# A hybrid decoder trunk in fp32 on one core: the order of ScalarE's work inside a slot, and of two masks on GpSimd

## The chip, the cores and the metric

The kernel runs on one core of one Trainium2 chip. The metric is the device time of one execution in microseconds (us), the median of some runs. Five engines with a queue each do the work: TensorE (PE in the profile; its weight loads are PEld), VectorE (DVE), ScalarE (ACT), GpSimd (POOL) and SyncE (SP), which here only issues DMAs. Each engine takes its instructions strictly in program order, and they wait for each other by semaphores: an instruction that waits holds back everything behind it on its own engine.

## The reference

Two layers over 256 tokens of width 1024. In each, one input projection feeds three mixers, and then comes a gated MLP:

```python
for l in range(DEPTH):                       # DEPTH = 2
    h = rms_norm(x, norm_mix[l])
    proj = h @ w_in[l]
    u_ssm, q_nsa, kv_nsa, g_nsa, qkv_sb, g_merge = split_columns(proj)
    o_ssm = s5_mixer(u_ssm, ...)             # A: complex diagonal state space, a scan over the tokens
    o_nsa = nsa_mixer(q_b, k_b, v_b, ...)    # B: softmax attention, compressed/selected/window branches
    o_sb  = stick_breaking_attention(...)    # C: see below
    gate = sigmoid(g_merge)                  # one gate of width 1024 for each mixer
    x = x + (sum(gate * (branches @ w_branch[l])) @ w_out[l])
    x = x + conv_ffn(rms_norm(x, norm_ffn[l]), ...)
return rms_norm(x, norm_final)

# mixer C, for each of 8 heads; causal is k < q
log_rest = where(causal, log_sigmoid(-z), 0)
after = cumsum(log_rest, reverse=True) - log_rest
w = where(causal, exp(log_sigmoid(z) + after), 0)
out = w @ v
```

## The kernel before

**Products in fp32 by halves.** A weight piece of 128 x 1024 numbers is split into a high half on ScalarE (`split_hi`, line 1278, `wh<-ring`) and the rest on VectorE (`split_lo`, line 1576, `wl<-ring,wh`). TensorE then multiplies high by high, high by low and low by high. A semaphore `w_lo` tells TensorE that a piece is there, `w_used` tells ScalarE that one of the three piece buffers is free again.

**Units and banks.** The results of the input projection come as units in two PSUM banks, `pj0` for even units and `pj1` for odd ones. ScalarE empties a bank with `copy_out` (line 1265), which raises `unit_out`; TensorE can't start the next unit in that bank before. The units named `sbv` and `gate` are "wide": two slots of TensorE's work each fill `pj0` and `pj1` together, so their two copies come only at the end of every fourth slot.

**Slots.** The middle of a layer is a loop `for q in range(SLOTS)` with 56 slots, written out in the same order for each engine. In a slot TensorE does one "filler" (a piece of the projection, 12 matmuls of 512 columns for a wide one; from slot 36 on half of that of the branch projections), and then what tables of slot numbers put there for the mixers. The tables that matter here:

- Mixer B: `NSA_S` scores on TensorE, one slot later `NSA_X` the maxima on VectorE (`nm`) and the exponentials on ScalarE (line 1367), then `NSA_R` the scaling (line 1378), `NSA_T` transposes on TensorE, `NSA_C` their copy on ScalarE.
- Mixer A (S5): `S5_X` inputs on TensorE, `S5_T` turns on VectorE and GpSimd, `S5_G` a scan on VectorE and `s5_back` on GpSimd (line 2169), `S5_Y` outputs on TensorE (line 1091), which wait for the `s5_back` of four groups.
- Mixer C works on four pairs of heads, k = 0 to 3. `SB_Z` (slots 25, 29, 34, 39): scores into `bA` and `bB`. `SB_A`, a slot later: Abs (line 1395), Exp (1398) and Ln (1400) on ScalarE. `SB_P`, again a slot later: the sum on VectorE (`kr<-bA,work`) and the first mask on GpSimd (`kr<-kr`, line 2177). `SB_R` (slots 28, 32, 38, 42): TensorE's cumulative sum (`bA<-kr,kon`). `SB_M`, a slot later: the exponential of the weights on ScalarE (line 1384). `SB_D`: the second mask, on the weights, on GpSimd (`work<-work`, line 2177). `SB_O` (slots 30, 34, 40, 44): values on TensorE (`pj<-work,sbv`), which wait for that mask.

In ScalarE's slot the order is: `split_hi`, the copies of mixer B, then the exponentials and scalings of mixer B, `SB_M`, `SB_A`, and last, in odd slots, the `copy_out` of a unit that has just been filled. In GpSimd's slot it is: first mask, second mask, turns, `s5_back`. The table of the second mask puts it in the slot of `SB_M`, and for k = 0 one slot earlier, in slot 28, which has an `s5_back` behind it:

```python
SB_M = {s + 1: k for s, k in SB_R.items()}
SB_D = {s - (k == 0): k for s, k in SB_M.items()}
```

ScalarE evaluates Exp and Tanh from one function table, Ln from another; an `ACT_TABLE_LOAD` stands where it changes between them.

Of the kernel before, what the change touches and what calls it, by code (L numbers as in the profile page):

```python
# [21 lines left out]
ACT = mybir.ActivationFunctionType  # L22
# [7 lines left out]
NT = T // P  # L30
EPS = 1e-6
HD = 64
SCALE = HD ** -0.5
# [66 lines left out]
U_VG, U_K, U_Q, U_U, U_FILL = 0, 2, 4, 6, 8  # L100
# [31 lines left out]
SB_M = {s + 1: k for s, k in SB_R.items()}  # L132
SB_O = {s + 2: k for s, k in SB_R.items()}

SB_D = {s - (k == 0): k for s, k in SB_M.items()}

S5_X = {4 + (7 * p + 1) // 2: p for p in range(ST // 2)}
S5_T = {s + 1: p for s, p in S5_X.items()}
# [86 lines left out]
def build(nc, x, norm_mix, w_in, ssm_lam_re, ssm_lam_im, ssm_log_step, ssm_b_re, ssm_b_im,  # L225
# [3 lines left out]
    with ExitStack() as ctx:  # L229
# [54 lines left out]
        sbq = sb("sbq", [P, JC, T])  # L284
        sbk = sb("sbk", [P, 4, T])
        sbv = sb("sbv", [P, NT, CH])
        gate = sb("gate", [P, 3 * KD, T])
# [242 lines left out]
        def half(h):  # L530
            return slice(CH * h, CH * h + CH)
# [701 lines left out]
        def _(a):  # L1233
# [26 lines left out]
            def copy_out(l, n, dst, func=ACT.Copy, scale=1.0):  # L1260

                t, k = summed(n)
                a.wait_ge(t.sem, t.at(l, k))
                src = unit(n) if len(dst.shape) == 3 else pj[n % 2][:, :]
                A(dst, src, func, scale=scale).then_inc(unit_out[n % 2].sem, unit_out[n % 2].up())  # L1265
# [16 lines left out]
            for l in range(DEPTH):  # L1282
# [61 lines left out]
                for q in range(SLOTS):  # L1344
# [7 lines left out]
                    if q in NSA_C:  # L1352
                        r = NSA_C[q]
                        m = ROUNDS[r]
                        a.wait_ge(t_done.sem, t_done.at(l, r + 1))
                        if m:
                            a.wait_ge(v_done.sem, v_done.at(l, m))
                        A(pT[:, r % 3 // 2, :], bO[:, :], ACT.Copy).then_inc(t_ready.sem, t_ready.up())
                    if q in NSA_X:
                        m = NSA_X[q]  # L1360
                        w = nsa_pair(m)[2]
                        a.wait_ge(s_max.sem, s_max.at(l, m + 1))
                        for s in range(2):
                            for b in range(2):
                                p = pr[:, m % 2, s, w * b:w * b + w]
                                n = 2 * s + b
                                ins = A(p, p, ACT.Exp, bias=nm[:, m % 2, n:n + 1], scale=-1.0,  # L1367
                                        accum_out=sm[:, m % 2, n:n + 1])
                        ins.then_inc(s_exp.sem, s_exp.up())
# [16 lines left out]
                    if q in SB_A:  # L1386
# [11 lines left out]
                        A(w, w, ACT.Exp, scale=-1.0).then_inc(z_exp.sem, z_exp.up())  # L1398
                        a.wait_ge(z_exp.sem, z_exp.at(l, k + 1))
                        A(w, w, ACT.Ln, bias=1.0).then_inc(z_ln.sem, z_ln.up())  # L1400
                    if q % 2:
                        kind, *at = FILL[f]
                        if kind == "sbq":
                            copy_out(l, U_FILL + f, sbq[:, 2 * at[0]:2 * at[0] + 2, :], scale=SCALE)
                        elif kind == "sbk":
                            copy_out(l, U_FILL + f, sbk[:, 2 * at[0]:2 * at[0] + 2, :])
                        elif kind == "sbv":
                            for t in range(at[0] * NT):
                                copy_out(l, U_FILL + f - 1 + t, sbv[:, t, :])
                        elif kind == "glu":  # L1410
                            o = oS[:, 2 * at[0]:2 * at[0] + 2, :]
                            copy_out(l, U_FILL + f, o, ACT.Tanh, 0.5)
                        elif kind == "gate":
                            b, i = at
                            for t in range(i % 2 * NT):
                                copy_out(l, U_FILL + f - 1 + t, gates[:, b, t, half(i // 2)], ACT.Tanh, 0.5)
                    if q == GELU:
                        a.wait_ge(y_used.sem, y_used.at(l, JC))
                        A(yT[:, :, :], yT[:, :, :], ACT.Gelu_apprx_tanh).then_inc(y_ready.sem, y_ready.up())
# [834 lines left out]
```

## Time and profile before

| | us |
|---|---|
| median of 3 runs | 988.85 (988.18 to 989.59) |
| profiled execution, its own time | 989.32 |
| its span, first to last instruction | 987.6 |
| busy: TensorE, VectorE, ScalarE, GpSimd | 948.0, 777.8, 590.2, 340.3 |

The profile is of one execution, whose time stands 0.5 us above the median. Times in its rows are microseconds from the span's start. Slot 12 of the first layer begins on TensorE at 121.6 us, that of the second at 603.7 us. TensorE is busy for 96% of the span, so what it waits for, and how fast its clock runs, is most of what can change the time. A wait is put down to the engine that came last.

### The profile page before, as it was taken

The numbers are of one execution on the slowest core, as the hardware profiler recorded it, in microseconds if no ns is written. First come the engines' busy times: TensorE is split into PE (matmuls) and PEld (weight loads), VectorE is DVE, ScalarE is ACT, GpSimd is POOL, SyncE is SP. The second block draws the span as 40 slices with busy tenths as digits, with TensorE's granted clock in tenths as the row PEclk, the third lists the DMA queues.
The fourth block names the chain that finished last, engine by engine and source line by source line (L and its number), as shares of the span: only waits on it lengthen the run. The fifth ranks groups of instructions, "written<-read, shape, count | busy, mean of one in ns | idle before, by whom it ended". The sixth has DMA issues, their size and how long they took to land. (4 is left out here: it accounts for less than half of the span.)

```text
span 987.6 us, 15962 instructions
## 1 busy us (share of the span) xinstructions
PE 948.0 (96%) x5743; PEld 782.8 (79%) x5743; DVE 777.8 (79%) x1284; ACT 590.2 (60%) x949; POOL 340.3 (34%) x267
## 2 busy tenths in 40 slices
PE   6899899999999999999999998999999999999997
PEld 6799676776877888888889986767677788888885
DVE  5989999996666878788965679899847668787776
ACT  6436666757455666666664466665765456565655
POOL 0111666772330483256501046567506000101010
PEclk9999999999999999999999998999999999999999
DMA  8963433345454756555468433332644436555551
GB/s 229 243 209 94 132 118 124 97 122 171 136 168 157 203 176 205 176 199 184 132 174 256 150 105 114 100 118 97 172 155 153 159 128 209 180 198 180 196 186 43
DMA packets 135863, 156.79 MB, mean 159 GB/s; under 512 B 16401, under 2 KB 103033, under 8 KB 135801
## 3 DMA queue, kind: packets, MB, share of 16 engines
q1 hardware_dynamic: 135800, 155.98, 50.3%
q8 instruction: 37, 0.61, 0.3%
q14 instruction: 26, 0.21, 0.1%
HBM read 154.92 MB, written 1.05 MB: 158 GB/s over the span
## 5 line engine op out<-in xcount | busy, mean ns | idle before, releaser
L1576 DVE TENSOR_TENSOR wl<-ring,wh 128x1024 fp32r<-128x1024 f32 (+1 forms) x276 | 366.1, 1329 | 76.0 <-ACT wh L1278 74.7
L1278 ACT ACTIVATE wh<-ring 128x1024 fp32r<-128x1024 f32 (+1 forms) x276 | 288.5, 1048 | 136.7 <-PE pj L744 105.0
L744 PE MATMUL pj<-h,wh 128*128 128x512 f32 (+1 forms) x1344 | 295.6, 342 | 7.8 <-DVE wl L1576 5.9
L744 PE MATMUL pj<-wh,h 128*128 128x512 f32 (+1 forms) x832 | 276.9, 399 | 10.2 <-ACT sbv L1265 4.9
L744 PEld LDWEIGHTS pj<-h,wh 128*128 128x128 f32 x1344 | 227.3, 190 | 36.7 <-issue 6.5
L744 PEld LDWEIGHTS pj<-wh,h 128*128 128x128 f32 x832 | 156.4, 190 | 57.0 <-issue 11.5
L744 PE MATMUL pj<-h,wl 128*128 128x256 f32 x1024 | 188.6, 282 | 0.0
L744 PEld LDWEIGHTS pj<-h,wl 128*128 128x128 f32 x1024 | 157.2, 191 | 6.9
L744 PE MATMUL pj<-wl,h 128*128 128x512 f32 (+1 forms) x416 | 160.9, 387 | 0.0
L2207 POOL TENSOR_TENSOR work<-work 128x512 f32<-128x512 f32 x20 | 41.0, 2049 | 287.5 <-DVE work L2025 191.5
L744 PEld LDWEIGHTS pj<-wl,h 128*128 128x128 f32 x416 | 79.3, 191 | 13.0
L2025 DVE SCALAR_TENSOR_TENSOR work<-pj,par,work 128x254 f32<-128x254 f32 (+1 forms) x176 | 76.7, 476 | 7.5 <-ACT work L1502 2.4
L1495 ACT ACTIVATE kr<-pj 128x512 f32<-128x512 f32 x44 | 26.3, 598 | 69.6 <-PE pj L744 69.6
L2015 DVE TENSOR_TENSOR pj<-pj,kr 128x512 f32<-128x512 f32 x44 | 30.7, 698 | 26.2 <-ACT kr L1495 26.0
L1502 ACT ACTIVATE work<-pj,par 128x256 f32<-128x256 f32 x88 | 44.9, 562 | 5.2 <-DVE pj L2015 4.7
L1367 ACT ACTIVATE work<-work,nm 128x128 f32<-128x128 f32 (+1 forms) x64 | 28.4, 445 | 29.7 <-DVE nm L1869 29.5
L2151 POOL TENSOR_TENSOR mr<-mr,work 128x512 f32<-128x512 f32 x16 | 31.8, 2004 | 32.7 <-DVE work L1634 32.7
L744 PE MATMUL bX<-wh,al 128*128 128x512 f32 x88 | 34.7, 394 | 0.0
L744 PE MATMUL bX<-wl,ah 128*128 128x512 f32 x88 | 34.5, 392 | 0.0
L744 PE MATMUL bX<-wh,ah 128*128 128x512 f32 x88 | 34.3, 389 | 0.0
L1378 ACT ACTIVATE work<-work,rg 128x128 f32<-128x128 f32 (+1 forms) x64 | 23.9, 444 | 16.2 <-DVE rg L1883 15.9
L1905 DVE TENSOR_TENSOR_SCAN bnat<-s5p,bnat 128x128 f32<-128x128 f32 x32 | 33.1, 1073 | 0.0
(313 smaller groups left out, 1417.7 us busy)
## 6 DMA issues: line engine op xcount, KB each, us to landing
ring<-in_ffn_w_up SPq DMA_DIRECT2D x44, 1024.0 KB, 5.1
ring<-in_w_in SPq DMA_DIRECT2D x40, 1024.0 KB, 5.1
ring<-in_ffn_w_down SPq DMA_DIRECT2D x22, 1024.0 KB, 4.9
ring<-in_w_in SPq DMA_DIRECT2D x16, 512.0 KB, 5.4
ring<-in_w_branch SPq DMA_DIRECT2D x8, 1024.0 KB, 5.0
ring<-in_w_out SPq DMA_DIRECT2D x8, 1024.0 KB, 5.1
ring<-in_w_branch SPq DMA_DIRECT2D x8, 512.0 KB, 5.8
ring<-in_w_in SPq DMA_DIRECT2D x8, 256.0 KB, 4.5
```

What stands on the lines that cost most here:

```text
L744: return nc.tensor.matmul(o, a, b, start=start, stop=stop, skip_group_check=True)
L1278: A(dst, src, ACT.Copy).then_inc(w_hi.sem, 1)
L1367: ins = A(p, p, ACT.Exp, bias=nm[:, m % 2, n:n + 1], scale=-1.0, accum_out=sm[:, m % 2, n:n + 1])
L1378: ins = A(p, p, ACT.Copy, scale=rg[:, m % 2, n:n + 1])
L1495: A(ups[n % 2], pjs[n % 2][:, :, T:2 * T], ACT.Copy).then_inc(lows_out.sem, 1)
L1502: ins = A(cv[:, e, T * m:T * m + T], pjs[n % 2][:, m, 0:T], ACT.Identity, bias=par[:, 2, bass.ds(tile + (C_B + m), 1)], scale=par[:, 2, ba ...
L1576: TT(dst, src, hi.bitcast(F32), ALU.subtract).then_inc(w_lo.sem, 1)
L1905: ins = nc.vector.tensor_tensor_scan(g, decay, g, s5i[:, 2 + c:3 + c] if b else 0.0, ALU.mult, ALU.add)
L2015: TT(o, o, ups[n % 2], ALU.add).then_inc(up_done.sem, 1)
L2025: ins = STT(dst, pjs[n % 2][:, m, 0:T - back], par[:, 1, bass.ds(tile + (col + m), 1)], dst, ALU.mult, ALU.add)
L2151: TT(m, m, yt[:, k % 2, :], ALU.add)\
L2207: TT(aT[:, cc % 2, :], cv[:, 0, :], cv[:, 1, :], ALU.mult).then_inc(a_ready.sem, 1)
```

## The change

Two edits. In ScalarE's loop over the slots the block that empties the unit's bank is moved from behind the exponentials and scalings to ahead of them, right behind the copies of `NSA_C`. And the table `SB_D` moves one mask of the weights by a slot: k = 0 goes back from slot 28 to 29, k = 1 comes forward from slot 33 to 32.

```diff
-SB_D = {s - (k == 0): k for s, k in SB_M.items()}
+SB_D = {s - (k == 1): k for s, k in SB_M.items()}
@@ ScalarE, in: for q in range(SLOTS)
                         A(pT[:, r % 3 // 2, :], bO[:, :], ACT.Copy).then_inc(t_ready.sem, t_ready.up())
+                    if q % 2:
+                        kind, *at = FILL[f]
+                        if kind == "sbq":
+                            copy_out(l, U_FILL + f, sbq[:, 2 * at[0]:2 * at[0] + 2, :], scale=SCALE)
...
+                        elif kind == "sbv":
+                            for t in range(at[0] * NT):
+                                copy_out(l, U_FILL + f - 1 + t, sbv[:, t, :])
...
+                        elif kind == "gate":
+                            b, i = at
+                            for t in range(i % 2 * NT):
+                                copy_out(l, U_FILL + f - 1 + t, gates[:, b, t, half(i // 2)], ACT.Tanh, 0.5)
                     if q in NSA_X:
...
                         A(w, w, ACT.Ln, bias=1.0).then_inc(z_ln.sem, z_ln.up())
-                    if q % 2:
-                        kind, *at = FILL[f]
...
```

TensorE's, VectorE's and SyncE's programs keep their order. On ScalarE the order differs in five slots of each layer: 7 (the copy of `sbk` now ahead of scaling 0), 11 (`sbv` ahead of exponentials 2), 19 (`gate` ahead of scaling 5), 23 (`gate` ahead of exponentials 7) and 35 (`gate` ahead of `SB_A` for k = 2).

In slot 11 ScalarE has before (`work,sm<-work,nm` are the exponentials, `sbv<-pj` the copies out of the two banks):

```order
L1358 ACTIVATE work<-pj 128x512
L1367 ACTIVATE work,sm<-work,nm 128x128 x4
L1265 ACTIVATE sbv<-pj 128x512 x2
L1278 ACTIVATE wh<-ring 128x1024
L1358 ACTIVATE work<-pj 128x512
```

and after the change:

```order
L1358 ACTIVATE work<-pj 128x512
L1265 ACTIVATE sbv<-pj 128x512 x2
L1383 ACTIVATE work,sm<-work,nm 128x128 x4
L1278 ACTIVATE wh<-ring 128x1024
L1358 ACTIVATE work<-pj 128x512
```

The two copies have passed the four exponentials (line numbers shift by 16).

In slots 35 to 39 ScalarE has before (`bA`, `bB` at L1395 begin `SB_A` for k = 2, those at L1384 are `SB_M` for k = 2):

```order
L1395 ACTIVATE work<-bA 128x384
L1395 ACTIVATE work<-bB 128x384
L1398 ACTIVATE work<-work 128x2x384
L1400 ACT_TABLE_LOAD
L1400 ACTIVATE work<-work 128x2x384
L1265 ACT_TABLE_LOAD
L1265 ACTIVATE gate<-pj 128x512 x2
L1278 ACTIVATE wh<-ring 128x1024 x2
L1384 ACTIVATE work<-bA 128x384
L1384 ACTIVATE work<-bB 128x384
```

and after the change:

```order
L1265 ACTIVATE gate<-pj 128x512 x2
L1411 ACTIVATE work<-bA 128x384
L1411 ACTIVATE work<-bB 128x384
L1414 ACTIVATE work<-work 128x2x384
L1416 ACT_TABLE_LOAD
L1416 ACTIVATE work<-work 128x2x384
L1278 ACTIVATE wh<-ring 128x1024 x2
L1400 ACT_TABLE_LOAD
L1400 ACTIVATE work<-bA 128x384
L1400 ACTIVATE work<-bB 128x384
```

The two gate copies now stand ahead of Abs, Exp and Ln, and the second table load stands in front of `SB_M` instead of in front of the gates.

On GpSimd, slots 27 to 33, before (`work<-work` is the mask of the weights, L2169 is `s5_back`, `kr<-kr` the first mask):

```order
L2169 TENSOR_TENSOR s5a<-s5x,tab 128x512 x2
L2177 AFFINE_SELECT work<-work 128x4x128
L2169 TENSOR_TENSOR mr<-bnat,tab 128x512 x2
L2161 TENSOR_TENSOR s5x<-mr 128x256
L2162 TENSOR_TENSOR s5x<-mr 128x256
L2161 TENSOR_TENSOR bnat<-s5h 128x256
L2162 TENSOR_TENSOR bnat<-s5h 128x256
L2177 AFFINE_SELECT kr<-kr 128x4x128
L2169 TENSOR_TENSOR mr<-s5x,tab 128x512 x2
L2169 TENSOR_TENSOR s5h<-bnat,tab 128x512 x2
L2177 AFFINE_SELECT work<-work 128x4x128
```

and after the change:

```order
L2169 TENSOR_TENSOR s5a<-s5x,tab 128x512 x2
L2169 TENSOR_TENSOR mr<-bnat,tab 128x512 x2
L2177 AFFINE_SELECT work<-work 128x4x128
L2161 TENSOR_TENSOR s5x<-mr 128x256
L2162 TENSOR_TENSOR s5x<-mr 128x256
L2161 TENSOR_TENSOR bnat<-s5h 128x256
L2162 TENSOR_TENSOR bnat<-s5h 128x256
L2177 AFFINE_SELECT kr<-kr 128x4x128
L2169 TENSOR_TENSOR mr<-s5x,tab 128x512 x2
L2177 AFFINE_SELECT work<-work 128x4x128
L2169 TENSOR_TENSOR s5h<-bnat,tab 128x512 x2
```

The first `work<-work` (k = 0) has gone behind one `s5_back`, the second (k = 1) ahead of one.

## Rows read from the trace of the kernel before

**Rows 1.** The page, busy time of each engine.
```profile
PE 948.0 (96%) x5743; PEld 782.8 (79%) x5743; DVE 777.8 (79%) x1284; ACT 590.2 (60%) x949; POOL 340.3 (34%) x267
```
**Rows 2.** Waits of TensorE: waiting <- waited for, us in total, times, longest.
```profile
PE pj L744 <- ACT sbv L1265: 4.9, 2, 2.4
PE pj L744 <- POOL work L2177: 3.2, 2, 1.6
...
PE pj L744 <- ACT gate L1265: 1.7, 4, 0.6
```
**Rows 3.** TensorE's timeline (start, duration, [idle before <-releaser]), slot 12, first layer.
```profile
121.57 0.77 PE L744 MATMUL pj<-wh,h 128*128 128x512 f32 x1 [2.44 <-ACT sbv L1265]
```
**Rows 4.** ScalarE's timeline, slot 11 of the first layer.
```profile
119.30 0.40 ACT L1367 ACTIVATE work<-work,nm 128x128 f32<-128x128 f32 x1 [3.89 <-DVE nm L1869]
...
120.86 1.05 ACT L1265 ACTIVATE sbv<-pj 128x512 f32<-128x512 f32 x2
```
**Rows 5.** Stretches: length, PE busy, granted clock (share of 2.4 GHz), DMA.
```profile
121.60:124.60 3.00, 3.00 (x7) 0.50 0.85 250
...
603.80:609.00 5.20, 5.20 (x12) 0.50 0.62 202
226.40:230.00 3.60, 3.60 (x44) 1.00 0.99 296
```
**Rows 6.** VectorE's timeline: the halves for slots 11 and 12, then its idle times.
```profile
112.69 3.14 DVE L1576 TENSOR_TENSOR wl<-ring,wh 128x1024 fp32r<-128x1024 f32 x2
...
142.25 0.29 DVE L1869 CUSTOM_DVE_ANT_0 work<-bA,kon 128x128 f32<-128x128 f32 x1 [1.91 <-PE bB L744]
...
610.60 0.42 DVE L1869 CUSTOM_DVE_ANT_0 work<-bA,kon 128x256 f32<-128x256 f32 x1 [0.67 <-PE bB L744]
...
616.92 0.48 DVE L1929 SCALAR_TENSOR_TENSOR uT<-uT,par,pj 128x256 f32<-128x256 f32 x1 [1.17 <-PE pj L1091]
...
625.51 0.29 DVE L1869 CUSTOM_DVE_ANT_0 work<-bA,kon 128x128 f32<-128x128 f32 x1 [2.61 <-PE bB L744]
```
**Rows 7.** TensorE's timeline at SB_R 0, SB_O 1, S5_Y 3, SB_R 2, SB_R 3.
```profile
198.03 1.04 PE L744 MATMUL bA<-kr,kon 128*128 128x256 f32 x6
...
226.37 0.87 PE L744 MATMUL pj<-work,sbv 128*64 128x256 f32 x8 [1.63 <-POOL work L2177]
227.17 0.40 PE L1091 MATMUL pj<-s5a,CL 128*32 128x256 f32 x1
...
235.96 1.04 PE L744 MATMUL bA<-kr,kon 128*128 128x256 f32 x6
...
246.14 1.14 PE L744 MATMUL bA<-kr,kon 128*128 128x256 f32 x6 [0.67 <-POOL kr L2177]
```
**Rows 8.** GpSimd's timeline: first mask of k = 0, the last s5_back.
```profile
196.73 0.75 POOL L2177 TENSOR_SCALAR_AFFINE_SELECT kr<-kr 128x512 f32<-128x512 f32 x1
...
220.86 4.41 POOL L2169 TENSOR_TENSOR s5h<-bnat,tab 128x512 f32<-128x512 f32 x2 [1.78 <-DVE bnat L1905]
```
**Rows 9.** ScalarE's timeline: SB_M 1, SB_A 2, slot 35's gates, SB_M 2, SB_A 3.
```profile
218.44 0.49 ACT L1384 ACTIVATE work<-bA 128x384 f32<-128x384 f32 x1 [0.64 <-PE bB L744]
...
224.98 0.47 ACT L1395 ACTIVATE work<-bA 128x384 f32<-128x384 f32 x1
...
226.72 1.28 ACT L1400 ACT_TABLE_LOAD   x1
228.02 0.84 ACT L1400 ACTIVATE work<-work 128x768 f32<-128x768 f32 x1
228.88 1.28 ACT L1265 ACT_TABLE_LOAD   x1
...
232.08 0.60 ACT L1265 ACTIVATE gate<-pj 128x512 f32<-128x512 f32 x1 [0.76 <-PE pj L744]
...
237.92 0.49 ACT L1384 ACTIVATE work<-bA 128x384 f32<-128x384 f32 x1 [1.98 <-PE bB L744]
...
240.34 0.47 ACT L1395 ACTIVATE work<-bA 128x384 f32<-128x384 f32 x1
```

More of the change, by code:

```diff
@@ L1358, in _ @@
                         A(pT[:, r % 3 // 2, :], bO[:, :], ACT.Copy).then_inc(t_ready.sem, t_ready.up())
+                    if q % 2:
+                        kind, *at = FILL[f]
+                        if kind == "sbq":
+                            copy_out(l, U_FILL + f, sbq[:, 2 * at[0]:2 * at[0] + 2, :], scale=SCALE)
+                        elif kind == "sbk":
+                            copy_out(l, U_FILL + f, sbk[:, 2 * at[0]:2 * at[0] + 2, :])
+                        elif kind == "sbv":
+                            for t in range(at[0] * NT):
+                                copy_out(l, U_FILL + f - 1 + t, sbv[:, t, :])
+                        elif kind == "glu":
+                            o = oS[:, 2 * at[0]:2 * at[0] + 2, :]
+                            copy_out(l, U_FILL + f, o, ACT.Tanh, 0.5)
+                        elif kind == "gate":
+                            b, i = at
+                            for t in range(i % 2 * NT):
+                                copy_out(l, U_FILL + f - 1 + t, gates[:, b, t, half(i // 2)], ACT.Tanh, 0.5)
                     if q in NSA_X:
@@ L1400, in _ @@
                         A(w, w, ACT.Ln, bias=1.0).then_inc(z_ln.sem, z_ln.up())
-                    if q % 2:
-                        kind, *at = FILL[f]
[L1403 to L1416, printed above, removed]
                     if q == GELU:
```

## The prediction, made blind

> **What bounds the kernel now.** I read four views. The page's busy times come first: TensorE works 948.0 of 987.6 us [rows 1], so only its waits and its clock leave anything to win, some 40 us in all. The view of waits tells which of them ScalarE and GpSimd cause: 4.9 us behind the copies of `sbv` (2 times 2.4), 3.2 behind the weights' mask (2 times 1.6) and 1.7 behind gate copies, the longest 0.6 [rows 2]. The timelines then show the instructions, and the windows the clock. Each wait comes once per layer; I work in the first layer's times and add the second where it differs.
>
> **The copies ahead of the exponentials, slot 11.** TensorE stood for 2.44 us before slot 12, until the first `sbv` copy had emptied its bank [rows 3], and as long in the second layer [rows 2]. ScalarE itself had waited 3.89 us for VectorE's maxima, then did four exponentials, and only from 120.86 the copies [rows 4]. With the copies first they fall into ScalarE's idle time. Nothing else is late: the halves for slot 12 were there at 112.69 + 3.14 = 115.8 [rows 6]. So 2.4 us go, in each layer. The exponentials wait for the maxima as before, so they lose nothing.
>
> The wait also cost clock. After it TensorE ran at 0.50, the level of 1.2 GHz, over the whole of 121.6 to 124.6 and again over 603.8 to 609.0, while after the 1.63 us wait at 226.4 it stayed at 1.00 [rows 5]. Half of 3.0 and of 5.2 us is 1.5 and 2.6 us more. TensorE alone would thus be 3.9 us ahead in the first layer and 5.0 in the second; the 0.6 behind the gates of slot 19 adds to both: 4.5 and 5.6. The copies moved in slots 7 and 23 remove no wait that the totals show over 0.3 us; I count zero for them.
>
> **How far TensorE may run ahead.** VectorE and GpSimd do the S5 scans meanwhile and hardly rest. VectorE's idle time from slot 12 to 34 that TensorE causes is 1.91 us in the first layer and 0.67 + 1.17 + 2.61 = 4.45 in the second [rows 6]; only by so much can its chain come forward. TensorE meets it at `SB_R` for k = 0, which began at 198.03 when the first mask had ended at 196.73 + 0.75 = 197.48 [rows 7, 8]: 0.55 to spare. So at slot 28 the lead is 1.91 + 0.55 = 2.5 us in the first layer and 4.45 + 0.55 = 5.0 in the second. Of 4.5 + 5.6 us that is 7.5; the rest turns into a wait for GpSimd.
>
> **The masks.** For k = 1 TensorE waited 1.63 us at 226.37, because the mask stood behind an `s5_back` of 4.41 us that began at 220.86 [rows 7, 8]. Its exponentials began at 218.44 and take some 0.9, so the mask could run at about 219.4, in GpSimd's 1.78 us of idle time, and `s5_back` starts as before. The wait goes. What is late next is the S5 output right behind: it needs that `s5_back`, which ended at 225.27, and began at 227.17 [rows 7, 8], 1.90 to spare. The lead behind slot 34 is the smaller of 2.5 + 1.63 and 1.91 + 1.90, so 3.8 us; in the second layer of 5.0 + 1.6 and 4.45 + 1.90, so 6.3. The mask for k = 0, now behind one `s5_back` more, has only TensorE's values of slot 30 as its reader. I count nothing; at most it pushes the turns behind it by the 0.75 us of a mask [rows 8] in each layer, and if GpSimd is early there it costs nothing.
>
> **The price, slot 35.** Here the moved copy does harm. The gate copies must wait for TensorE to finish slot 35: the second began at 232.08 after 0.76 us of waiting [rows 9]. Before, Abs, Exp and Ln for k = 2 filled that wait: they began at 224.98 [rows 9]. Now they queue behind the copy, and begin at 232.08 + 0.60 less a slight overlap, 232.6, 7.6 us later. Who waits: VectorE's sum, GpSimd's first mask, then `SB_R` on TensorE, three half slots after slot 35, at 235.96 [rows 7]. The chain's length stands in the trace for k = 3, where nothing hides it: from Abs at 240.34 to `SB_R` at 246.14 [rows 7, 9], 5.8 us. So 232.6 + 5.8 = 238.4, and TensorE stands for 2.4 us. This counts from TensorE's own end of slot 35, so no lead shortens it. It is 2.4 in each layer, 4.8 in all. The `split_hi` of slot 36 comes 4 us later, too; its piece is first used in slot 40, so I count nothing.
>
> Whether the clock falls after this wait is not in the trace. The nearest rows are 2.44 us, after which it fell both times, and 1.63, after which it did not [rows 3, 5, 7]. From both sides: 0, or 2 x 2.6 = 5.2. I take one fall of two, at the mean of 1.5 and 2.6: 2.1 us.
>
> **The table load.** One load per layer moves from ahead of the gates to ahead of `SB_M` of k = 2. It takes 1.28 us and does not wait for what its activation waits for: at 228.88 it began as Ln ended, with the gates still waiting behind it [rows 9]. In the changed order Ln ends at 232.6 + 3.9 = 236.5 (3.9 being 224.98 to 228.86), and the exponentials can't begin before `SB_R` is through, 2.0 us after its start as before (235.96 to 237.92), so at 240.4 [rows 7, 9]. The 3.9 us between hold two `split_hi` and the load. I count nothing, and 1.28 in each layer if that cover were gone. The Trainium skill (ScalarE: Activation LUTs, "What ACT_TABLE_LOAD costs") has a switch cost the load and a drain, 2.66 us together. The trace speaks against a drain here: the load at 226.72 ended at 228.00 and Ln began at 228.02 [rows 9]. By the rule the sum would be up to 1.4 us a layer worse, less the cover that is left.
>
> **The sum.** Lead 3.8 + 6.3 = 10.1; price 4.8; clock 2.1. Net 3.2 us less. The profiled execution took 989.3, so it would take 986.1; the median stands 0.5 below it, which gives 985.6.
>
> **The rivals.**
> *TensorE's lead is lost.* VectorE and GpSimd share the S5 chain, whose pace (the `s5_back` at 220.86 took 4.41 us [rows 8]) is not TensorE's to set. If that chain comes forward by nothing but its idle time and the 0.55 and 1.90 to spare melt away, the lead is 1.9 + 4.45 = 6.4. Against 4.8 and 2.1 that is 0.5 us more: 989.35 for the median. For it: VectorE is at 79% over all and nearly without pause in these slots. Against: it is ahead of TensorE by whole pieces there. Chance 0.18.
> *Slower: Abs, Exp and Ln behind the gates.* The mechanism is the wait at `SB_R` of k = 2, with the clock falling in both layers for as long as in the second layer before. Price 4.8 + 5.2 = 10.0; with the smaller lead of 6.4 it is 3.6 more: 992.5. It decides if the clock falls after this wait each time and the lead stays below 8. For it: 2.4 us is almost the 2.44 that cost clock twice. Chance 0.12.
> *The price is not paid*, because the chain from Abs is shorter when VectorE and GpSimd are free of S5 work, or because the lead survives whole: 10.1 to 12 us less and a price of at most 2, no fall of the clock: 980. Against: k = 3's chain was measured with both of them free. Chance 0.05.
> *The change doesn't do all that it says:* the copies of slot 11 late for another reason, so that half of the lead of one layer, 2 to 3 us, is missing: 988. Chance 0.05. The rule of the longer switch would end at the same place or below.
>
> **How the numbers follow.** My forecast has a chance of 0.60. Its own range goes from no fall of the clock (10.1 - 4.8 = 5.3 less, 983.5) to two long ones (0.1 more, 989.0), with 985.6 in the middle. The range of all, 982.8 to 989.8, leaves out the unpaid price at 980 and the slower case. A difference under 0.2%, 2 us, can't be told from none. Faster than 986.9: four fifths of the forecast (0.48), all of the unpaid price (0.05), and 0.07 of the lost lead and the last together, 0.60. Slower than 990.8: the slower case and a little beside, 0.12. The same: 0.28.
>
> **What would show it.** In the changed profile the wait of TensorE for `sbv` is gone from the view of waits, and the windows at slot 12 show clock 1.00. VectorE's idle times before slot 16 have shrunk. `SB_R` of k = 0 has a new wait of 1 to 2 us in the first layer, released by GpSimd. The wait for `work` at `SB_O` of k = 1 is gone. A wait of about 2.4 us for `kr` stands at `SB_R` of k = 2, in both layers. ScalarE's Abs for k = 2 stands right behind a gate copy. I am wrong if that wait is under 1 us, or if the lead ahead of slot 35 is not 3.8 and 6.3; then the step on how far TensorE may run ahead has failed.

## The result: 0.2% slower, where 0.3% faster was forecast

| | us |
|---|---|
| kernel before, median of 20 runs | 988.33 |
| changed kernel, median of 20 runs | 990.09 (989.32 to 993.98) |
| ratio | 1.0023, 95% interval 1.0015 to 1.0031 |
| forecast | 985.6, range 982.8 to 989.8 |
| profiled execution of the changed kernel: its own time, span | 991.54, 989.8 |

The time lies above the range. The profiled execution is 1.5 us slower than the median of its kernel, and that of the kernel before (989.32) 1.0 us slower than its own. Both differences turn out to be slow clock, below; so sizes are read from traces, and the sum is held against medians. Two executions of 2368 us, one of the kernel before and one of the kernel with the masks alone, stand apart from all the others and are left out of the ratios.

### The profile page after: what moved, and what is told of

It is laid out like the page before. It is cut to its first block and busy times, and to the rows that moved or that the text cites. A ratio compares the mean times of both kernels' runs of the same rounds, so it can differ in the third digit from the quotient of the medians.

```text
span 989.8 us, 15962 instructions
## 1 busy us (share of the span) xinstructions
PE 947.8 (96%) x5743; PEld 783.6 (79%) x5743; DVE 779.1 (79%) x1284; ACT 589.0 (60%) x949; POOL 342.7 (35%) x267
## 5 line engine op out<-in xcount | busy, mean ns | idle before, releaser
L744 PE MATMUL pj<-wh,h 128*128 128x512 f32 (+1 forms) x832 | 274.1, 396 | 4.6 <-DVE wl L1576 3.0
```

The source lines that it names most:

```text
L744: return nc.tensor.matmul(o, a, b, start=start, stop=stop, skip_group_check=True)
```

## The profile after

Waits of TensorE (waiting <- waited for, us in total, times, longest), against [rows 2]:

```profile
PE pj L744 <- DVE wl L1576: 10.5, 14, 1.4
PE bA L744 <- POOL kr L2177: 7.5, 4, 3.1
...
PE pj L744 <- issue: 3.1, 2, 1.6
...
PE pj L744 <- ACT work L1358: 1.8, 2, 0.9
```

The 4.9 us for `sbv` and the 3.2 for the weights' mask are gone, as the change says. In their place stand 3.1 us twice for the first mask (`kr`), and two waits that the prediction did not have: one of 1.6 (in slot 14) that no releaser is shown for, and one of 0.9 (in slot 24) for a copy on ScalarE, each once per layer. The wait of 1 to 2 us for GpSimd that the prediction expected at `SB_R` of k = 0 is not among them.

TensorE's timeline at `SB_R` 0, the S5 output behind `SB_O` 1, `SB_R` 2 and `SB_R` 3, against [rows 7]:

```profile
195.94 1.14 PE L744 MATMUL bA<-kr,kon 128*128 128x256 f32 x6
...
223.98 0.40 PE L1091 MATMUL pj<-s5a,CL 128*32 128x256 f32 x1 [0.41 <-POOL s5h L2169]
...
236.05 1.83 PE L744 MATMUL bA<-kr,kon 128*128 128x256 f32 x5 [3.11 <-POOL kr L2177]
...
247.97 1.14 PE L744 MATMUL bA<-kr,kon 128*128 128x256 f32 x6 [0.65 <-POOL kr L2177]
```

Against these rows TensorE is 2.1 us ahead at the first, 3.2 at the second, level at the third and 1.8 us behind at the fourth. The first two hold the gain and the last two hold the loss. What made the wait of 3.11 is on the three other engines. ScalarE, slots 11 and 35 to 37, against [rows 4, 9]:

```profile
116.36 0.60 ACT L1265 ACTIVATE sbv<-pj 128x512 f32<-128x512 f32 x1 [0.76 <-PE pj L744]
...
228.90 0.60 ACT L1265 ACTIVATE gate<-pj 128x512 f32<-128x512 f32 x1 [0.77 <-PE pj L744]
229.39 0.49 ACT L1411 ACTIVATE work<-bA 128x384 f32<-128x384 f32 x1
...
231.16 1.28 ACT L1416 ACT_TABLE_LOAD   x1
232.45 0.84 ACT L1416 ACTIVATE work<-work 128x768 f32<-128x768 f32 x1
```

VectorE, the sum for k = 2 and what follows it:

```profile
233.33 0.56 DVE L1945 SCALAR_TENSOR_TENSOR kr<-bA,work 128x384 f32<-128x384 f32 x1 [5.39 <-ACT work L1416]
233.80 0.55 DVE L1945 SCALAR_TENSOR_TENSOR kr<-bB,work 128x384 f32<-128x384 f32 x1
234.28 1.23 DVE L1576 TENSOR_TENSOR wl<-ring,wh 128x1024 fp32r<-128x1024 f32 x1
```

GpSimd, the second mask of k = 1, `s5_back`, the first masks of k = 2 and 3:

```profile
217.51 0.75 POOL L2177 TENSOR_SCALAR_AFFINE_SELECT work<-work 128x512 f32<-128x512 f32 x1
219.53 4.40 POOL L2169 TENSOR_TENSOR s5h<-bnat,tab 128x512 f32<-128x512 f32 x2 [1.26 <-DVE bnat L1905]
234.52 1.48 POOL L2177 TENSOR_SCALAR_AFFINE_SELECT kr<-kr 128x512 f32<-128x512 f32 x1 [10.59 <-DVE kr L1945]
...
247.28 0.63 POOL L2177 TENSOR_SCALAR_AFFINE_SELECT kr<-kr 128x512 f32<-128x512 f32 x1 [5.84 <-DVE kr L1945]
```

Abs for k = 2 stands directly behind the gate copy that waits for TensorE's end of slot 35, as predicted. Four steps on, the first mask of k = 2 took 1.48 us where that of k = 3 took 0.63: a `split_lo` runs on VectorE at that moment. From Abs to `SB_R` it is 236.05 - 229.39 = 6.66 us, not the 5.8 of k = 3.

Windows (stretch, length, busy time of PE, PEld, DVE, ACT and POOL, granted clock, DMA) at slot 12, over the wait, and behind it in each layer, against [rows 5]:

```profile
118.00:125.00 7.00, 7.00 (x51) 4.84 (x48) 6.86 (x20) 3.84 (x13) 4.18 (x3) 1.00 0.52 166
232.90:236.00 3.10, 0.04 (x1) 0.00 (x0) 2.67 (x4) 3.08 (x4) 1.48 (x1) 1.00 0.00 0
236.10:240.00 3.90, 3.90 (x14) 3.49 (x15) 1.13 (x1) 0.63 (x2) 0.00 (x0) 0.56 0.40 91
719.90:724.00 4.10, 4.10 (x16) 3.58 (x17) 1.12 (x1) 1.26 (x3) 0.18 (x1) 0.61 0.34 100
```

The clock is back at slot 12. It now falls behind slot 37, in both layers (0.56 and 0.61).

## The experiments

The theory (A in the expectations): all of the loss is made at slot 35, wait plus clock, about 5 us per layer in the traces; the leads elsewhere are real. The rival (B): the leads do not reach the end, since VectorE and GpSimd set the pace. Ratios are to the kernel before, run beside each on the same chip. The positions used below are those of TensorE, counted from its S5 inputs of slot 11 in the same layer (117.42 and 599.58 in the trace of before).

**Slot 35 late again**

```diff
-                    if q % 2:              # ahead of the exponentials
+                    if q % 2 and q != 35:
 ...
+                    if q == 35:            # behind SB_A, as before the change
+                        (the same copies)
```

> The changed kernel, but the gate copies of slot 35 alone stand again behind Abs, Exp and Ln of k = 2. Theory A (the loss is made at slot 35 alone: in the changed trace TensorE waits 3.1 us at SB_R of k = 2 and then runs SB_R to SB_Z in 4.99 instead of 3.24 us, so about 5 us per layer, while the leads of 3.4 and 4.5 us behind slot 34 are real): the wait for kr is back at 0 or under 1 us, no fall of the clock at slot 38, and the time is 988.3 - 7.9 = 980.4. Theory B (the leads do not survive, since VectorE and GpSimd set the pace of the rest anyway): 986 to 989. By the prediction's own leads of 3.8 and 6.3: 988.3 - 10.1 = 978.2.

982.12 us, ratio 0.9932 (0.9920 to 0.9945). By its ratio this is the fastest of the full kernels run, 8.0 us below the changed kernel by the medians (9.0 by the ratios), and its five times span 0.4 us. So the loss is at slot 35, and the rest of the change is a gain of 6.2 us (6.7 by the ratio), somewhat less than A's 7.9.

**Slot 35 alone**

```diff
+                    if q == 35:            # added to the kernel before
+                        (gate copies ahead of SB_A)
```

> The kernel before, with slot 35's gate copies alone moved ahead of Abs, Exp and Ln of k = 2: the price by itself. Theory A: a wait of 3.2 us and 1.75 us of slower clock per layer, 9.9 in all: 998.2. The prediction's sizes (2.4 per layer, and one fall of the clock of 2.1): 988.3 + 6.9 = 995.2. Theory B (the price is mostly hidden, and the changed kernel lost its leads elsewhere): 988 to 991.

997.79 us (994.73 to 1000.85), ratio 1.0092 (1.0072 to 1.0112): 9.5 us more by the medians and 9.1 by the ratio, close to the 9.9 of theory A. TensorE's wait has the same size without any lead in front of it:

```profile
239.07 0.48 PE L744 MATMUL bA<-kr,kon 128*128 128x256 f32 x1 [3.11 <-POOL kr L2193]
```

This bears out the prediction's sentence that no lead shortens the wait. The mean granted clock of the six executions goes with their times: 0.995 and 0.994 for the three up to 996.6, 0.990 and 0.988 for the three above. The slow clock is what varies.

**The masks alone**

```diff
-SB_D = {s - (k == 0): k for s, k in SB_M.items()}
+SB_D = {s - (k == 1): k for s, k in SB_M.items()}
```

> The kernel before with the new table SB_D alone. The wait of 1.63 us at SB_O of k = 1 goes in both layers and nothing comes in its place, since the S5 output behind it has 1.90 us to spare: 988.3 - 3.2 = 985.1. Theory B (the masks' new order pushes GpSimd's turns and the gain comes back as another wait): 987.5 to 989.

986.68 us, ratio 0.9976 (0.9967 to 0.9986): 2.4 us by the ratio and 1.7 by the medians, of 3.2. The wait for the weights' mask is gone in both layers; of each 1.6 us, 0.3 comes back as a wait for `s5h` right behind it, and some 0.25 as waits for gates (2.2 us in all, of 1.7 before). At `SB_R` of k = 3 TensorE is 0.8 to 0.9 us ahead of the first layer before, in both layers. "`s5_back` starts as before" did not hold. GpSimd, and the instruction of VectorE that ran beside the mask:

```profile
219.75 0.63 POOL L2193 TENSOR_SCALAR_AFFINE_SELECT work<-work 128x512 f32<-128x512 f32 x1 [0.35 <-ACT work L1400]
221.65 4.41 POOL L2185 TENSOR_TENSOR s5h<-bnat,tab 128x512 f32<-128x512 f32 x2 [1.26 <-DVE bnat L1921]
```

```profile
219.72 0.69 DVE L1928 TENSOR_SCALAR s5i<-ends,bnat 128x2 f32<-128x2 f32 x1
```

`s5_back` began at 221.65, 0.5 later than in [rows 8] once the 0.26 us between the two traces' origins are taken off. The trace shows why: the mask now runs beside a small instruction on VectorE that belongs to the scan for which `s5_back` waits. It took 0.69 us, where it took 0.23 (at 219.40) before.

**The copies alone, without slot 35**

```diff
-                    if q % 2:
+                    if q % 2 and q != 35:  # SB_D as in the kernel before
```

> The kernel before with all moved copies early except slot 35's, and the masks as before. TensorE's 2.44 us and its slow clock at slot 12 go (3.9 and 5.0 us), but the mask of k = 1 still stands behind its s5_back, so the lead at slot 34 can be no more than what GpSimd's chain has come forward. Theory A: about 2 us in the first layer and 3 in the second, 983.3, and a wait for the mask at SB_O of k = 1 of 1.6 to 2.5 us. Theory B: all of it lost there, 987 to 989. If the two edits simply added, e4 and the masks alone would together give the time of the changed kernel with slot 35 late.

985.76 us, ratio 0.9973 (0.9961 to 0.9985). The wait at `SB_O` of k = 1 has grown to 1.86 and 1.82 us. Copies 2.6 and masks 1.7 us by these medians, 6.2 together: the masks' edit is worth 3.6 behind the copies. Two parts can be read. Without it the lead of the copies is cut at that mask, and at `SB_R` of k = 3 TensorE stands at 126.71 in the first layer instead of 125.71, so some 2 us in two layers. And the grown wait costs clock, which the theories had not counted: behind the 1.82 us of the second layer the windows show 0.64 (last section), and five of the six executions have a mean clock of 0.997, where slot 35 late has 0.999.

**TensorE kept busy through the wait at slot 35**, first with 26 matmuls of the identity, then with 13 (the profile shows two records for each)

```diff
+                    if q == 38:
+                        pe.wait_ge(x5_used.sem, x5_used.at(l, ST))
+                        idle(26, bX[0])        # 13 in the second
                     if q in SB_R:
                         sb_rest(SB_R[q])
```

> The changed kernel, with 26 matmuls of the identity into a bank that is free, put on TensorE ahead of SB_R for k = 2: the wait for GpSimd's first mask stays as it is, but TensorE works through nearly all of it. Nothing of the reference's computation is left out. If the price is 3.1 us of wait and 1.75 of clock per layer, the granted clock stays at 1.00 through slots 38 to 40 and only the wait is left: 982.1 (the version without the price, whose clock was at 0.999 over all) + 2 x 3.1 = 988.3, with a spread under 1 us instead of the 989.3 to 994.0 of the changed kernel. If the slow clock comes from something else than TensorE's standing still, the time stays at 990 and the window behind it at 0.5.

992.88 us, ratio 1.0049 (1.0035 to 1.0064). My size was wrong: the 26 took 5.97 us, longer than the wait, so this time says little. The clock stayed at 1.00. Hence the second:

> The changed kernel with 13 instead of 26 matmuls of the identity ahead of SB_R for k = 2; with 26 they took 5.97 us and lasted 2.6 us longer than the wait in each layer. The wait of 3.1 us stays, TensorE works through it, the clock stays up: 992.9 - 2 x 2.6 = 987.7, with a spread under 1 us. The difference to the changed kernel, 990.1, is the clock's part of the price, 2.4; that to the version with slot 35 late, 982.1, is the wait's, 5.6. If idle matmuls are no cure: 990.

988.52 us (988.05 to 988.83), ratio 1.0000 (0.9991 to 1.0009). TensorE's timeline and the windows of the second:

```profile
232.92 3.06 PE L745 MATMUL bX<-kon 128*128 128x128 f32 x26
236.19 1.14 PE L745 MATMUL bA<-kr,kon 128*128 128x256 f32 x6 [0.20 <-POOL kr L2197]
```

```profile
236.00:240.00 4.00, 3.81 (x22) 3.15 (x24) 1.66 (x3) 1.80 (x4) 0.77 (x2) 1.00 0.31 74
...
719.00:724.00 5.00, 5.00 (x31) 3.83 (x29) 2.27 (x3) 3.00 (x6) 0.64 (x1) 1.00 0.57 208
```

`SB_R` begins no earlier, but TensorE stands still for only 0.20 us ahead of it, and the clock does not fall. The 8.0 us between the changed kernel and the one with slot 35 late divide into 1.6 of clock (990.1 - 988.5; 2.4 were expected) and 6.4 of wait; by the ratios it is 2.3 and 6.7.

**VectorE's `split_lo` held back until the mask is done**

```diff
+                    if q == 36:
+                        v.wait_ge(z_spm.sem, z_spm.at(l, 3))
                     if q in SPLIT_AT:
                         split_lo(l, SPLIT_AT[q])
```

> The changed kernel, with VectorE's split_lo of slot 36 held back until GpSimd's first mask of k = 2 is done. In the changed kernel the two ran at once and the mask took 1.48 us; the mask of k = 3, with VectorE idle, took 0.64. If VectorE's split stretches the mask, it takes 0.64 here and the wait at SB_R falls from 3.1 to 2.3 us in both layers: 990.1 - 1.7 = 988.4, and as low as 985 if the clock then stays up. If the mask was long for another reason, it stays near 1.5, and the time is the same or up to 1 us longer, since the piece of slot 36 is late.

986.80 us (986.38 to 988.47), ratio 0.9989 (0.9981 to 0.9998), 3.3 below the changed kernel. GpSimd's mask, and TensorE in each layer:

```profile
234.42 0.64 POOL L2195 TENSOR_SCALAR_AFFINE_SELECT kr<-kr 128x512 f32<-128x512 f32 x1 [10.60 <-DVE kr L1961]
```

```profile
235.11 0.59 PE L744 MATMUL bA<-kr,kon 128*128 128x256 f32 x1 [2.27 <-POOL kr L2195]
```

```profile
718.33 0.48 PE L744 MATMUL bA<-kr,kon 128*128 128x256 f32 x1 [2.27 <-POOL kr L2195]
```

```profile
235.20:239.00 3.80, 3.80 (x14) 3.39 (x15) 2.85 (x3) 1.47 (x2) 0.00 (x0) 0.55 0.00 0
718.40:722.00 3.60, 3.60 (x22) 2.93 (x24) 3.02 (x4) 2.24 (x4) 0.58 (x1) 1.00 0.00 0
```

VectorE's split stretches the mask. Without it the wait is 2.27, close to the 2.4 that the prediction worked out. In this trace one of two such waits cost clock, but its execution, at 988.47, was the slowest of twelve. Four of them (988.1 to 988.5) have a mean clock of 0.996, the other eight (986.4 to 987.3) one of 0.998 or 0.999, and their times leave next to nothing for the clock: 982.1 + 2 x 2.27 = 986.7. So the 0.84 us on the mask cost twice: of the 3.3 us, 1.7 are wait (twice 0.84), and the other 1.6, an estimate by difference, are clock, as much as all that the 13 matmuls gave back.

**TensorE kept busy through the wait at slot 12, in the kernel before**

```diff
+                    if q == 12:
+                        idle(10)
                     filler(q)
```

> The kernel before, with 10 matmuls of the identity into a free part of bY on TensorE ahead of slot 12, which fill most of its 2.44 us wait for the copies of sbv (one such matmul took 0.23 us). The wait stays, only the standing still goes. If the slow clock behind that wait is due to TensorE's standing still, the windows at slot 12 show 1.00 in both layers, and the clock's own part of the gain is seen alone: in the changed kernel's trace and in this one's before it was 1.5 and 2.6 us, so 988.3 - 4.1 = 984.2 by the prediction's terms, or 985 if the 2.6 was a long one; all of it should reach the end, since it is less than the 2.5 us by which TensorE may come forward in a layer. If the lead does not survive: 986 to 988.

985.32 us (985.09 to 985.70), ratio 0.9972 (0.9962 to 0.9982).

```profile
121.60:124.60 3.00, 3.00 (x14) 2.24 (x16) 2.86 (x9) 2.02 (x4) 0.91 (x2) 1.00 0.82 251
...
603.80:609.00 5.20, 5.20 (x38) 3.48 (x37) 5.13 (x13) 2.84 (x7) 4.21 (x3) 1.00 0.44 170
```

With the wait for `sbv` still in place, its clock alone is worth 3.2 us by the medians (2.8 by the ratio). In the traces it is 1.5 and 2.6 us at `SB_R` of k = 0, still that at `SB_R` of k = 3, and the spans differ by 4.0: all of it reaches the end. The medians show less than the prediction's 4.1; the 2.6 of the second layer was a long one. In the trace with the masks alone the same 5.2 us show 0.75, half the loss.

**Slot 23's gates late as well**

```diff
-                    if q % 2 and q != 35:
+                    if q % 2 and q not in (23, 35):
```

> As the version with slot 35 late, and slot 23's gate copies late as well. In that version (982.1) TensorE waited 0.88 us in slot 24 of each layer for a copy of bO on ScalarE, which stood behind exponentials 7, and these behind the gate copies' waits for TensorE; before the change this wait was not there, and the lead fell from 3.2 to 2.3 us at that place. Theory A (this is where the lead was cut): the wait goes, and 0.9 us per layer come back, less 0.1 to 0.3 for the bank of the gates: 982.1 - 1.4 = 980.7. The prediction's theory (the lead is capped at slot 28 by the S5 chain of VectorE and GpSimd): a new wait at SB_R of k = 0 takes it back, 982.1.

982.38 us, ratio 0.9943 (0.9928 to 0.9957). No gain, and TensorE comes 0.5 us later to `SB_R` of k = 3 in each layer; my theory of this wait was wrong. ScalarE and TensorE:

```profile
173.90 0.51 ACT L1383 ACTIVATE work<-work,nm 128x256 f32<-128x256 f32 x1 [1.04 <-DVE nm L1885]
```

```profile
176.61 0.47 PE L744 MATMUL pj<-wh,h 128*128 128x512 f32 x1 [1.24 <-ACT gate L1265]
```

The exponentials wait for VectorE's maxima whichever order ScalarE has, and the 0.88 us turned into 1.24 for the gates behind them. It points to VectorE.

**Maxima ahead of a split; then bank `bY` emptied ahead of a scan**

```diff
+                    if q == 12:                # first run: slot 13's maxima
+                        nsa_max(NSA_X[13])     # ahead of slot 12's split_lo,
+                                               # and no longer in slot 13
                     if q in SPLIT_AT:
                         split_lo(l, SPLIT_AT[q])
+                    if q == 13:                # second run: the S5 output of
+                        (uT<-pj of slot 14)    # slot 13 ahead of its scan, and
+                                               # no longer in slot 14
                     if q in S5_G:
                         s5_scan(S5_G[q])
```

> As the version with slots 23 and 35 late, and VectorE takes the maxima of pair 3 (slot 13) ahead of slot 12's split_lo. TensorE waits 1.56 us in slot 14 for a copy of bO that stands on ScalarE behind exponentials 3, which wait for these maxima; they stood behind a split_lo of 1.22. If this order on VectorE sets that wait, it falls to about 0.4, and 1.2 us come back in each layer: about 2.4 below the version with slots 23 and 35 late, 978.3. Against it: the low half of slot 14's piece comes 1.4 us later, with only 0.6 to spare, so up to 0.8 per layer may come back as a wait for wl: 979.9. By the prediction's theory of the S5 chain nothing is gained.

982.73 us, ratio 0.9948 (0.9935 to 0.9960), with slots 23 and 35 late. The wait in slot 14 stayed at 1.56: it was never for the copy behind the exponentials. The version with slot 35 late shows what it was, TensorE and VectorE:

```profile
133.89 0.44 PE L744 MATMUL pj<-pcT,vc 128*64 128x128 f32 x4 [1.56 <-issue]
```

```profile
132.56 0.86 DVE L1921 TENSOR_TENSOR_SCAN s5x<-s5p,s5i,s5x 128x128 f32<-128x128 f32 x2
133.34 0.46 DVE L1945 SCALAR_TENSOR_TENSOR uT<-uT,par,pj 128x256 f32<-128x256 f32 x1
```

> The version with slot 35 late, and VectorE empties bY (the S5 output of slot 13) ahead of slot 13's scan instead of behind it. In that version TensorE waits 1.56 us in slot 14 with its operands there: bY is free only when VectorE's uT<-pj at 133.34 is through, behind a scan of 2.6 us. Taking VectorE's maxima earlier did nothing to it. If bY is what TensorE waits for, the wait falls to 0.3 (the copy of bO) and TensorE is 1.2 us further ahead at slot 16; whether that lasts tells of the cap. Cap by VectorE's chain as the prediction has it: the lead at slot 28 stays what it was and the time is 982 to 982.5. No cap: 982.1 - 2.4 = 979.7.

982.03 us, ratio 0.9943 (0.9929 to 0.9958), with slot 35 late only. TensorE, and what the second wait hangs on (VectorE's sum and GpSimd's mask for k = 0):

```profile
132.84 0.44 PE L744 MATMUL pj<-pcT,vc 128*64 128x128 f32 x4 [0.40 <-ACT work L1358]
```

```profile
195.71 1.14 PE L744 MATMUL bA<-kr,kon 128*128 128x256 f32 x6 [0.93 <-POOL kr L2197]
```

```profile
191.55 0.54 DVE L1961 SCALAR_TENSOR_TENSOR kr<-bB,work 128x384 f32<-128x384 f32 x1
```

```profile
194.90 0.75 POOL L2197 TENSOR_SCALAR_AFFINE_SELECT kr<-kr 128x512 f32<-128x512 f32 x1
```

It was `bY`, and the wait fell to 0.40. But at `SB_R` of k = 0 TensorE then waited 0.93 us for GpSimd and began 78.27 us behind the S5 inputs of slot 11, where it had begun at 78.34 before this edit. The sum was ready at 192.09, and the mask began 2.8 us later, directly behind GpSimd's turns. The time is unchanged: the prediction's cap, seen directly.

**Half of GpSimd's `s5_back`** (on top of the last; half of the S5 states are not turned back)

```diff
-                    for c in range(2):
+                    for c in range(1):
                         ins = TT(s5as[s % 6][:, c, :]..., gs, tab[:, c, ...], ALU.mult)
```

> The version with slot 35 late and bY emptied early, with one of the two products of every s5_back on GpSimd left out (so half of the S5 states are not turned back). In that version (982.0) TensorE gains 1.2 us at slot 14 and gives 0.9 of it back as a wait for GpSimd at SB_R of k = 0, and it waits 0.4 us at the S5 output behind SB_O of k = 1. If GpSimd's and VectorE's S5 chain caps the lead, a chain with some 2 us less work on GpSimd per group lifts the cap: both waits go, and the time falls by 2 x (0.9 + 0.4) to 979.4 or lower. If the cap is something else (VectorE's own queue, the copies on ScalarE), the waits stay and the time is 981.5 to 982.

976.78 us, ratio 0.9877 (0.9861 to 0.9894). The waits at `SB_R` of k = 0 and at the S5 output are gone, and `SB_R` of k = 0 begins at 76.70. The time is 5.3 us less by the medians and 6.5 by the ratios, at least twice the 2.6 of the two waits. VectorE gained too, without an instruction less: its busy time fell from 778.8 to 750.8 us, GpSimd's from 342.5 to 281.8. GpSimd's work stretches VectorE's, as the split stretched the mask above. So the cap is in the S5 work that the two share; how much of it is GpSimd's own time and how much VectorE's longer instructions, this run does not divide.

**Slot 11 and the masks, slots 7, 19 and 23 as before**

```diff
-                    if q % 2:
+                    if q == 11:
```

> The kernel before with slot 11's copies early and the new table SB_D, all other copies as before. Against the version that also moves the copies of slots 7, 19 and 23 (982.1) the wait of 0.65 us at slot 19 is back. By separate terms: 982.1 + 1.3 = 983.4. If VectorE's chain caps the lead behind slot 24 anyway, that wait costs nothing, and the wait of 0.88 us in slot 24 goes in exchange: 982.1 within 0.4.

983.17 us, ratio 0.9951 (0.9937 to 0.9966), 1.0 above the version with these three moved as well (1.9 by the ratios, whose intervals overlap): nearer to the 1.3 of separate terms than to the 0.4 of a full cap. `SB_R` of k = 0 begins at 78.87 in the first layer, 0.5 later. With slot 19's gates late, TensorE's wait for them there is 1.44 us.

## Why the prediction was wrong

TensorE's positions in the traces, in us behind its S5 inputs of slot 11, first and second layer:

| | `SB_R` 0 | S5 output behind `SB_O` 1 | `SB_R` 3 |
|---|---|---|---|
| before | 80.61, 81.77 | 109.75, 110.90 | 128.72, 129.90 |
| changed | 78.33, 78.37 | 106.37, 106.42 | 130.36, 130.38 |
| changed, slot 35 late | 78.34, 78.41 | 106.38, 106.47 | 125.71, 125.82 |
| slot 35 alone | 80.48, 80.74 | | 133.56, 134.90 |

**Copies of slot 11: right.** The wait of 2.44 and the slow clock went in both layers.

**The cap on the lead: right in kind, wrong in the second layer's size.** The step that failed is "VectorE's idle time from slot 12 to 34 that TensorE causes is 1.91 us in the first layer and 0.67 + 1.17 + 2.61 = 4.45 in the second [rows 6]; only by so much can its chain come forward." At `SB_R` 0 the lead was 2.3 us of the 2.5 predicted in the first layer, but 3.4 of 5.0 in the second. Nor did TensorE lose the rest where the prediction said, in a wait for GpSimd at `SB_R` of k = 0: it lost it earlier, mainly in slot 14 behind VectorE's scan (1.6 us), and the wait for GpSimd appeared only once that one was taken away. The windows over slots 11 to 34 of the kernel before:

```profile
118.00:226.00 108.00, 103.39 (x650) 75.73 (x646) 103.72 (x198) 71.00 (x143) 75.73 (x56) 0.98 0.40 119
600.20:709.00 108.80, 104.52 (x650) 76.36 (x646) 102.18 (x197) 70.69 (x142) 74.45 (x56) 0.97 0.38 115
```

and of the version with slot 35 late:

```profile
118.00:223.00 105.00, 102.30 (x656) 74.95 (x654) 103.25 (x196) 68.64 (x140) 75.07 (x56) 1.00 0.38 116
596.80:702.00 105.20, 102.48 (x658) 74.98 (x654) 102.83 (x196) 68.73 (x141) 75.27 (x56) 1.00 0.39 116
```

The busy times are those of PE, PEld, DVE, ACT and POOL. In the kernel before, nearly the same work took VectorE 1.5 us less in the second layer than in the first. TensorE was later there, VectorE stood idle more, and beside GpSimd's pauses its instructions were shorter (one `split_lo` of slot 14 took 2.19 in the first layer and 1.20 in the second). Brought forward, both layers run alike, with VectorE busy for 103 of 105 us. Up to the first mask of k = 0 the 4.45 us can be followed, in the second layer before and with slot 35 late:

```profile
600.20:680.70 80.50, 77.38 (x488) 55.88 (x485) 74.85 (x160) 53.80 (x119) 52.95 (x41) 0.96 0.34 109
```

```profile
596.80:674.40 77.60, 75.11 (x490) 54.43 (x486) 75.78 (x159) 52.17 (x118) 54.06 (x41) 1.00 0.35 113
```

```profile
640.16 1.74 DVE L1921 TENSOR_TENSOR_SCAN s5x<-s5p,s5x 128x128 f32<-128x128 f32 x2 [0.63 <-POOL s5x L2178]
```

The mask ended 81.22 us behind the S5 inputs of slot 11 before and 78.36 now, so the chain came forward by 2.9. VectorE is busy 0.9 us longer (75.78 for 74.85), and it has a new wait of 0.6 for GpSimd; together that is 4.4 of the 4.45. Idle time on one of two engines that stretch each other is not all to be had. The table also shows both layers of the changed versions at nearly the same position: the S5 chain's pace, not TensorE's. That the layers differed in the kernel before, by 1.2 us at `SB_R` 0, was one execution's clock: with the masks alone changed, the positions there are 80.60 and 80.64, and VectorE's long idle time is 1.93 and 1.90. From 80.64 the second layer's lead is 2.3, the same as the first's, and by the prediction's own rule it would have been 2.5 in both. So the rule is near the truth for executions like that one, and the 4.45 that it was fed came from a single one with a long fall of the clock.

**The masks: nearly right.** Beyond `SB_R` 0 they added 1.1 and 1.0 us, where the prediction had 1.3 and 1.3. Behind the S5 output the leads were thus 3.4 and 4.4 (slot 35 late), of 3.8 and 6.3; 7.8 in all instead of 10.1. By the medians the version without slot 35's price kept 6.2. Of the difference, some 0.7 goes behind slot 34 (3.0 and 4.1 at `SB_R` 3), and about 1.0 is the profiled execution of before, that much slower than its median. The prediction had taken off only 0.5 for that. Counted from an ordinary execution instead, with 2.5 in both layers at `SB_R` 0, the prediction's rule gives 3.8 twice, 7.6. This is an estimate, but it shows that some 2.5 of the 3.9 us missing in the lead came from the second layer's idle time.

**The price: right place, too small.** "So 232.6 + 5.8 = 238.4, and TensorE stands for 2.4 us" took the chain from k = 3, where VectorE has nothing behind its sum. For k = 2 a `split_lo` stands there, and the mask took 1.48. The chain was 6.66 and the wait 3.11. The trace of before had such a mask to show, that of k = 1:

```profile
212.01 1.46 POOL L2177 TENSOR_SCALAR_AFFINE_SELECT kr<-kr 128x512 f32<-128x512 f32 x1 [0.30 <-DVE kr L1945]
```

The sentence "k = 3's chain was measured with both of them free" stood among the rivals as an argument against a shorter chain; it was the reason to expect a longer one. The Trainium skill (SBUF — State Buffer, "SBUF: two separate sides") says that a VectorE operation with two inputs in SBUF and a GpSimd operation that reads SBUF hold one pair of ports by turns, the later one being blocked for the whole of the other. The rows agree in kind: the mask began 0.24 us behind the split and lasted 0.49 us beyond its end, where a mask alone takes 0.63.

**The clock: near in size, by luck.** The prediction took 2.1 us for waits of 2.4. In the trace of after, with waits of 3.11, the clock fell in both layers and cost 1.7 in each (`SB_R` to the scores of k = 3 took 4.99 and 4.96 us instead of 3.24). But twelve of the twenty executions (989.3 to 990.4) have a mean clock of 0.996 or 0.997, where the profiled one has 0.995 and slot 35 late 0.999, so the median pays for about one fall (an estimate): 1.6 us in both layers together, 2.3 by the ratios. For waits of 2.27, the nearest to those predicted, it pays next to nothing by the medians (986.8 against 986.7) and 1.1 by the ratios. The term was too large for the wait as predicted, and the longer wait made up for it. With the wait that makes 8.0, where the prediction had 6.9.

**Table load: right.** The load ahead of `SB_M` ran at 235.21, beside TensorE's wait, and nothing waited for it. Nothing stands between the load and Ln after the change either: 231.16 + 1.28 = 232.44, and Ln began at 232.45.

The sum: predicted 10.1 of gain and 6.9 of price, 3.2 less; measured by medians 6.2 of gain and 8.0 of price, 1.8 more. Of the 5.0 us between them 3.9 are the lead and 1.1 the price; the forecast is only 4.5 off, since it started from an execution that was 1.0 and not 0.5 above its median. (The prediction's "two long ones (0.1 more, 989.0)" has a wrong sign: 10.1 - 4.8 - 5.2 is 0.1 less, 988.75. The measured 990.1 is outside either way.) The rival "slower: Abs, Exp and Ln behind the gates", given 0.12, named the mechanism. Its lead of 6.4 is near the measured 6.2, its price of 10.0 is 2.0 above the measured 8.0. It deserved more: of its two conditions the lead under 8 came true, and the fall of the clock in both layers did in the profiled execution.

## What to carry to other kernels

A block that waits for the engine which sets the pace must not be moved ahead of a chain that leads back to that engine; here the same move paid in slot 11, gave 1.0 us in slots 7, 19 and 23 together, and cost 8.0 in slot 35. Leaving that one out gave 982.1 us, faster than both kernels. The length of such a chain is taken from where its engines have the same neighbours, since 0.84 us of one mask lay in what VectorE did beside it. Idle times, too, are taken from more than one execution, since a single long fall of the clock in the second layer more than doubled VectorE's. Idle time of an engine that shares work with another is an upper bound for what can come forward, and a lead has to be followed to every place where the slower chain hands over: here at a PSUM bank in slot 14, where the prediction looked at slot 28.

## What the runs showed of the hardware

- Standing still and the slow clock, in the traces here: after 3.11 us the clock fell to 0.5 each of four times, after 2.43 to 2.45 each time, after 2.27 once of two, after 1.82 and 1.86 once of two, and behind waits of 1.54 to 1.65 never. The traces are one execution each: the mean clocks of the changed kernel's other executions speak for fewer falls after 3.11 us than its trace shows. The fall is due to the standing still and not to the wait: with idle matmuls in the waits of 3.11 and 2.44 the clock stayed at 1.00. The fall after 1.82, in the version with the copies alone:

```profile
224.30:229.00 4.70, 4.70 (x49) 3.11 (x50) 2.38 (x5) 3.85 (x5) 0.00 (x0) 1.00 0.79 228
704.30:709.00 4.70, 4.67 (x42) 2.31 (x43) 0.75 (x2) 3.58 (x4) 0.00 (x0) 0.64 0.76 232
```

- What a fall costs differs between executions: behind the same wait of 2.44 us in the second layer the same 5.2 us show 0.50 in the kernel before and 0.75 with the masks alone. The falls go with most of the spread: five times within 0.4 us where the clock's mean is 0.999, 989.3 to 994.0 for the changed kernel with means of 0.997 down to 0.992. The Trainium skill (TensorE: Matmul & The Clock Gate, "What's actually happening") calls the number of slow matmuls at the start of a kernel variable from run to run; the rows here show the same for falls in its middle.
- Thirteen matmuls of the identity, 3.06 us, kept the clock at 1.00 through a wait. They cost at most 0.1 us: `SB_R` of k = 2 begins 118.53 us behind the S5 inputs of slot 11 with them and 118.44 without.
- An idle time with "issue" as its releaser was a wait for a bank that VectorE had to empty.
